# Gate-up weights by quarters of their columns, a later long convolution, decays and betas by transfers, and TensorE's usual end without a jump

## What is computed

```python
a = _rmsnorm(x, norm_mix);  proj = a @ w_in                      # q k v, z, beta, a, glu, gates
# branch a: gated delta rule, 8 heads, per token
beta = sigmoid(beta_raw);  g = -exp(a_log) * softplus(a_raw + dt_bias)
gc = cumsum(g) in chunks;  decay = exp(gc_i - gc_j);  kb = k * beta
# branch b: depthwise convolution with 31 taps over 512 channels, layernorm, silu
x = x + (g_a * branch_a + g_b * branch_b) @ w_out
# mixture of experts, 32 experts, top 4 for each token
for e in range(N_EXPERTS):
    gu = hm @ w_gate_up[e] + b_gate_up[e]                        # 1024 x 2048
    gate = jnp.minimum(gu[:, :D_FF], 7.0);  up = jnp.clip(gu[:, D_FF:], -7.0, 7.0)
    hid = (up + 1.0) * (gate * jax.nn.sigmoid(1.702 * gate))
    out = out + gates[:, e:e+1] * (hid @ w_down[e] + b_down[e])   # 1024 x 1024
x = x + out
x = x + (p_l @ w_ple_proj) * sigmoid(_rmsnorm(x, norm_ple) @ w_ple_gate)
y = _rmsnorm(x, norm_final)
```

## Time and profile before

| | |
|---|---|
| median of 3 runs | 1425.36 us (1422.98 to 1426.63) |
| profiled execution | 1425.09 us, its span 1423.0 us |
| PE busy | 1331.9 us (94%) |
| DVE, ACT, POOL busy | 456.7, 283.5, 27.9 us |
| moved | 463.23 MB, 326 GB/s over the span |

### The profile page before, as it was taken

How to read it: one execution, slowest core, us unless ns; L and a number is a source line. 1 busy time by engine, 2 the same in 40 slices (tenths; PEclk the granted TensorE clock), 3 DMA queues, 4 the chain that set the end, 5 groups by cost and what they waited for, 6 DMA issues and landing times.

```text
span 1423.0 us, 21274 instructions
## 1 busy us (share of the span) xinstructions
PE 1331.9 (94%) x8377; PEld 750.6 (53%) x8377; DVE 456.7 (32%) x1075; ACT 283.5 (20%) x609; POOL 27.9 (2%) x68
## 2 busy tenths in 40 slices
PE   8999899999999999999989889898898989989987
PEld 6877676778885443543433425334243443535455
DVE  3666868662235120220211202112020220202224
ACT  4645453534022100100100001000010000101024
POOL 3000000000000000000000000000000000000000
PEclk9999999999999999999999999999999999999999
DMA  7425244554868999999999999999999999999941
GB/s 219 138 90 154 91 125 148 152 209 126 323 217 351 402 420 422 420 421 420 422 420 420 421 422 421 421 421 421 421 421 421 420 415 420 421 422 421 419 154 31
DMA packets 123131, 463.23 MB, mean 326 GB/s; under 512 B 11141, under 2 KB 70046, under 8 KB 75310
## 3 DMA queue, kind: packets, MB, share of 16 engines
q1 hardware_dynamic: 106837, 452.99, 79.8%
q10 hardware_dynamic: 16193, 8.84, 2.2%
HBM read 455.78 MB, written 6.68 MB: 325 GB/s over the span
## 4 chain that ended last, share of the span: by engine, by line
PE 63%; DMA 15%; SPq 11%; DVE 5%; issue 3%; ACT 2%; ACTq 0%; POOL 0%; DVEq 0%; POOLq 0%
PE bank L1213 16%; PE bank L1260 12%; DMA ring<-in_w_gate_up 12%; SPq L622 11%; PE bank L1020 10%; PE bank L1152 5%; PE bank L1281 4%; PE bank L1067 3%; PE bank L1101 2%; PE bank L1335 2%; DMA late<-in_w_gate_up 2%; DMA dedicated<-in_w_gate_up 2%; PE bank L1199 1%; DVE lent L2010 1%; PE bank L1238 1%
## 5 line engine op out<-in xcount | busy, mean ns | idle before, releaser
L1213 PE MATMUL bank<-ring,lent 128*64 128x512 f32 (+1 forms) x1832 | 379.1, 595 | 44.1 <-DMA ring<-in_w_gate_up 44.1
L1213 PEld LDWEIGHTS bank<-ring,lent 128*64 128x64 f32 (+1 forms) x1832 | 121.8, 131 | 275.7 <-issue 275.2
L1020 PE MATMUL bank<-lent,ring 128*128 128x264 f32 x896 | 229.0, 397 | 5.1 <-DVE big L2030 1.6
L1260 PE MATMUL bank<-ring,lent 128*64 128x512 f32 (+1 forms) x928 | 184.3, 595 | 0.0
L1020 PEld LDWEIGHTS bank<-lent,ring 128*128 128x128 f32 x896 | 161.7, 191 | 40.4 <-issue 10.2
L2182 DVE TENSOR_SCALAR big<-bank 128x512 f32<-128x512 f32 x32 | 20.6, 686 | 409.2 <-PE bank L1213 409.2
L1260 PEld LDWEIGHTS bank<-ring,lent 128*64 128x64 f32 (+1 forms) x928 | 56.4, 129 | 106.8 <-issue 101.3
L1692 ACT ACTIVATE big<-big 128x512 f32<-128x512 f32 x32 | 19.5, 630 | 468.0 <-DVE big L2182 468.0
L1152 PEld LDWEIGHTS bank<-st,big 88*128 88x128 f32 x768 | 87.0, 192 | 13.6 <-issue 12.2
L1152 PE MATMUL bank<-st,big 88*128 88x128 f32 x768 | 90.3, 277 | 0.6 <-ACT pair_space L1689 0.5
L2200 DVE TENSOR_TENSOR xT<-xT,bank 128x264 f32<-128x264 f32 x128 | 55.0, 429 | 101.8 <-PE bank L1281 100.3
(11 more groups left out here) (436 smaller groups left out, 1352.3 us busy)
## 6 DMA issues: line engine op xcount, KB each, us to landing
ring<-in_w_gate_up SPq DMA_DIRECT2D x205, 1024.0 KB, 21.8
ring<-in_w_down SPq DMA_DIRECT2D x100, 1024.0 KB, 23.5
ring<-in_w_in SPq DMA_DIRECT2D x28, 1024.0 KB, 5.6
dedicated<-in_w_gate_up SPq DMA_DIRECT2D x13, 1024.0 KB, 23.8
dedicated<-in_w_down SPq DMA_DIRECT2D x9, 1024.0 KB, 24.1
late<-in_w_gate_up SPq DMA_DIRECT2D x8, 1024.0 KB, 23.0
outputs<-in_w_gate_up SPq DMA_DIRECT2D x7, 1024.0 KB, 26.4
lent<-in_w_gate_up SPq DMA_DIRECT2D x7, 1024.0 KB, 23.6
```

What stands on the lines that cost most here:

```text
L1020: last = mm(b[:, 0:T], w[:, k, o:o + P], aT[:, k, :], start=k == 0, stop=k == KD - 1)
L1213: last = mm(bank[t][lo:hi, :], x_slots[:, c, lo:hi], w, start=False, stop=c == KD - 1)
L1260: last = mm(bank[4 + t][lo:hi, :], hT[:, m, lo:hi], w, start=m == 0, stop=m == KD - 1)
```

## The change

1. **Quarters.** The host lays `w_gate_up` out so that chunk c = 2q + half holds, for four blocks of 128 contraction rows, the 256 gate and 256 up columns of quarter q. The chunk is still 1 MB, in rows of 8 KB. Chunk pair c now adds into bank q only, and quarter q is complete after two pairs. DVE and ACT work on quarters of 256 columns as they become complete, and PE transposes them between the pairs (`hidden_rows`). The scatter of the previous group moves from behind the gather to behind pairs 0 and 1. In the first group `x_ready` 2 is awaited at c = 1, not at c = 4.
2. **Places.** The first quarter's values are written early, so the two once-used places now hold chunks 2 and 3, and chunks 12 and 13 lie in the ring.
3. **Decays and betas.** `bcast` and `sel8` are gone. ACT stores the rows to DRAM once (slot 19) and reads them back spread over the partitions, two transfers for each pair of heads, issued in slot 24 and, for the next pair, in step `dt4` (`spread_rows`).
4. **Long convolution.** Taps come at 1 a slot up to slot 96 and at 2 a slot from there, its mean is asked for in slot 150 (`CONF_END` 50).
5. **End of PE.** The condition is turned round: the usual case is the body of the If, with `last_scatter` and the gate products (`ending`) in it. The last scatter uses eight different banks and starts when the first half of the last outputs is copied.
6. POOL clears `DT` and `Dm` for g < 2 only. `keep_warm` in the last group shrinks from 9 products to 2.

```diff
-BEFORE = {20: [17], 21: [18], 25: [3, 4], 26: [7, 8], 32: [0, 1], 33: [2, 5], 34: [6, 19]}
+BEFORE = {20: [17], 21: [18], 25: [13, 4], 26: [7, 8], 32: [0, 1], 33: [12, 5], 34: [6, 19]}
-SCATTER_BANKS = [4, 5, 6, 7, 2, 3, 6, 7]
+SCATTER_BANKS = [4, 5, 6, 7, 4, 5, 6, 7]
+LAST_BANKS = [1, 6, 7, 0, 2, 3, 4, 5]
-CONF_ROWS, TAILS, CONF_END = 22, 51, 48
+CONF_ROWS, TAILS, CONF_END = 22, 51, 50
-TAPS_FROM = 14
+TAPS_FROM, TAPS_DENSE_FROM = 14, 96
-        due += 4
+        due += 3 if x < TAPS_DENSE_FROM else 6
+        for i, name in zip((2, 3), ONCE):
+            j = home_of.index(name)
+            home_of[i], home_of[j] = home_of[j], home_of[i]
@@ PE, a group @@
+                    q, half = divmod(c, 2)
+                    for k in range(4):
                         for i, (x, lo, hi) in enumerate(tiles):
-                            w = weights(sems, n, 2 * c + x, t * 512)
-                            last = mm(bank[t][lo:hi, :], x_slots[:, c, lo:hi], w, start=False, stop=c == KD - 1)
+                            w = weights(sems, n, 2 * c + x, k * 512)
+                            last = mm(bank[q][lo:hi, :], x_slots[:, 4 * half + k, lo:hi], w, start=False,
+                                      stop=half == 1 and k == 3)
+                    if not first and c < 2:
+                        if c == 0:
+                            pe.wait_ge(sm["y_ready"], n * 2)
+                        scatter(sm, n - 1, 4 * c, 4 * c + 4)
...
+                    if half == 1 and c > 1:
+                        hidden_rows(sm, n, q - 1)
...
+                if not first:
+                    pe.wait_ge(sm["sc_added"], n * KD)
                 if not last_one:
                     gather(sm, n + 1)
                 elif end:
-                    pe.wait_ge(sm["y_ready"], n * 2)
-                    keep_warm(bank[4], 9)
+                    keep_warm(bank[4], 2)
+                hidden_rows(sm, n, 3)
+                gated_by_slot(sm, n)
@@ PE, the end @@
-            with pe.If(most > CAP):
+            with pe.If(most < CAP + 1):
                 last_scatter(first, GROUPS)
+                ending()
+            with pe.Else():
...
@@ ACT @@
+            def spread_rows(g):
+                betas = work[g % 2][10]
+                act.wait_ge(rows_stored, 16)
+                if g:
+                    act.wait_ge(s["sscaled"], 2 * g)
+                    act.wait_ge(s["kbg_ready"], 2 * g)
+                if g >= 2:
+                    wait_drained(act, f"o.{g - 2}")
+                for dst, x, done in ((eg, 1, decays_spread), (betas, 0, betas_spread)):
+                    src = head_rows[2 * g:2 * g + 2, x, :].unsqueeze(0).broadcast_to([P, 2, T])
+                    act.dma_start(dst, src).then_inc(done, 16)
-                    for j in range(2):
-                        b = to_drain(act, name(f"bcg{j}"))
-                        act.wait_ge(s["dec_diff"], 4 * g + 2 * j + 2)
-                        out_of(A(eg[:, j, :], b[:, 0:T], ACT.Exp), name(f"bcg{j}"))
+                    act.wait_ge(s["dec_diff"], 4 * g + 4)
+                    tell(A(eg[:], eg[:], ACT.Exp))
@@ DVE, a group @@
+                for q in range(4):
+                    g, u, gs = quarter(gbuf, q), quarter(ubuf, q), quarter(gsig, q)
+                    dve.wait_ge(sm["chunk_used"], at * RING + 4 * (q + 1))
+                    v.tensor_scalar(g, bank[q][:, 0:QUARTER_COLS], LIMIT, None, ALU.min).then_inc(sm["gate_in"], 1)
+                    then(v.tensor_scalar(u, bank[q][:, QUARTER_COLS:512], LIMIT, -LIMIT, ALU.min, ALU.max))
+                    dve.wait_ge(sm["gate_sig"], n * 4 + (q + 1))
+                    then(v.tensor_tensor(gs, gs, g, ALU.mult))
+                    v.scalar_tensor_tensor(g, u, 1.0, gs, ALU.add, ALU.mult).then_inc(sm["hid"], 1)
```

More of the change, by code:

```diff
@@ L1284, in last_scatter @@
             def last_scatter(sm, end):
-                pe.wait_ge(sm["y_ready"], end * 2)
                 pe.wait_ge(sm["spread"], end)
-                pe.wait_ge(sm["sc_added"], (end - 1) * KD)
-                scatter(sm, end - 1, 0, 6)
-                pe.wait_ge(sm["sc_added"], (end - 1) * KD + 4)
-                scatter(sm, end - 1, 6, 8)
+                pe.wait_ge(sm["h_ready"], end * 4)
+                pe.wait_ge(s["bd_added"], KD)
+                for i in range(KD):
+                    if i in (0, 4):
+                        pe.wait_ge(sm["y_ready"], end * 2 - (1 if i == 0 else 0))
+                    mm(bank[LAST_BANKS[i]][:, 0:T], y[:, i * P:(i + 1) * P], spread,
+                       start=True, stop=True).then_inc(sm["sc_filled"], 1)
             def gates_to_rows():
@@ L1536, in gdn_step @@
                     out_of(x, name(step))
+                    if step == "dt4" and g < 3:
+                        spread_rows(g + 1)
                 elif step == "adl":
@@ L2173, in group @@
                     make_selector(sm, eye_order, after, pos + 2)
+                if not first:
+                    add_back(sm, n - 1, SCATTER_BANKS)
                 if end:
-                    dve.wait_ge(sm["sc_added"], n * KD - KD)
-                    for i in range(KD):
-                        dve.wait_ge(s["bd_filled"], i + 1)
-                        v.tensor_tensor(xT[:, i, :], xT[:, i, :], bank[6 + i % 2][:, 0:T], ALU.add).then_inc(s["bd_added"], 1)
-                    dve.wait_ge(s["bd_added"], KD)
@@ L2190, in group @@
-                assert own[0] == PER
-                if not first:
-                    add_back(sm, n - 1, 0, KD)
+                    dve.wait_ge(sm["sc_added"], n * KD)
+                for q in range(4):
+                    g, u, gs = quarter(gbuf, q), quarter(ubuf, q), quarter(gsig, q)
[5 more added lines that the diff above has]
+                    v.scalar_tensor_tensor(g, u, 1.0, gs, ALU.add, ALU.mult).then_inc(sm["hid"], 1)
+                    if end:
+                        for i in (2 * q, 2 * q + 1):
+                            dve.wait_ge(s["bd_filled"], i + 1)
+                            v.tensor_tensor(xT[:, i, :], xT[:, i, :], bank[6 + i % 2][:, 0:T], ALU.add).then_inc(s["bd_added"], 1)
@@ L2194, in group, with add_back @@
+                assert own[0] == PER
+                if end:
+                    dve.wait_ge(s["bd_added"], KD)
                 dve.wait_ge(sm["pt_filled"], n + 1)
                 v.tensor_copy(spread, bank[2][0:SLOTS, 0:T]).then_inc(sm["spread"], 1)
[L2197 to L2198 removed]
+            def add_back(sm, n, banks):
+                for i in range(KD):
                     dve.wait_ge(sm["sc_filled"], n * KD + (i + 1))
[L2200 removed]
+                    v.tensor_tensor(xT[:, i, :], xT[:, i, :], bank[banks[i]][:, 0:T], ALU.add).then_inc(sm["sc_added"], 1)
```

273 lines of the change are left out of this document (125 added, 148 removed).

## The result

The changed kernel takes 1438.5 us (median of 4 runs, 1437.4 to 1442.1) against 1425.1 us, a ratio of 1.0095 with an interval of 1.0083 to 1.0107. It is 13.4 us slower, where 6.8 us faster was forecast. Its profiled execution takes 1439.2 us with a span of 1437.5 us, 14.5 us more than the span of before.

A forecast was written before the change was run, and what follows sets the result against it. Transfers were taken to set the experts' pace, about 59.8 us a group. Terms -8.6 + 2.8 - 0.9 = -6.7 us took the span from 1423.0 to 1416.3, forecast 1418.6 us, range 1413.5 to 1423.5 for 8 in 10.

The forecast's parts named there:

- (a): When PE starts on the experts counts in full, since all places are full and DMA waits for PE to free one.
- (b): Idle DMA time in the first expert group, before the queue has built up, counts in full.
- The first group, +2.8: Opening expert group: 4.1 us of added DMA idle time, less a 1.3 us gap that goes; bounds +1.5 and +4.1.
- The 4.1 us for pair 1: Opening group: pair 1 frees no place, so the next issues wait 3.6 us for pair 2, plus 0.5 us.
- The short gap at 476 to 480 us: First group: a DMA gap worth 1.3 us should go, as chunks 12 and 13 now free places.
- The first part, -0.9: Work ahead of the experts, with 32 PE instructions gone and taps moved: -0.9 us, bounds -7.1 and +3.
- PE will only wait longer: First part: with its products removed PE waits longer for ACT; gain 0.2 us for the first pair, 0 for the others.
- The taps: Long convolution in the first part: fewer early taps -0.8 us, mean not waiting -0.7, denser taps in slots 120 to 129 +0.7.
- The end, -8.6: Behind the last expert transfer: gate products start at 1370.9 in place of 1379.5, with the last w_ple_gate chunk as the floor.
- Half clock at the gate products: Rival: PE idles before the gate products and its clock falls, +2.4 us, 1421.0; chance 0.18.
- PE's removed work counts: Rival in the first part: ACT was itself held by PE, so up to 7.1 us go; half gives 1415; chance 0.12.
- PE's group passes the pace of the transfers: Rival: scatter and transposes between pairs lengthen each of some 15 groups; 8 us a group gives +22, 1441; chance 0.04.

The follow-up runs named there:

- experiment 6: Changed kernel with opening group's transposes behind its pairs, rows spread by products and the old long-convolution timetable: 1424.8 us, ratio 0.9994 to the kernel before.
- Experiment 1: Changed kernel, but in the opening group the first three quarters' transposes stand behind the eighth gate-up pair: 1429.2 us, ratio 1.0038 to the kernel before.
- experiment 2: Changed kernel plus 12 unread DVE operations, 5 us in all, behind the ordering of the experts: 1442.1 us.
- experiment 3: Changed kernel with decays and betas spread by 16 PE products again, no transfers for them: 1434.6 us, ratio 1.0077 to the kernel before.
- experiment 4: Changed kernel, rows still spread by transfers, plus unread PE products of the removed products' size in their old slots: 1434.0 us, ratio 1.0056 to the kernel before.
- experiment 8: Kernel before plus quarters and new ending, the opening group's first two transposes ahead of the gather: 1421.7 us, ratio 0.9974 to the kernel before.
- experiment 9: Kernel of experiment 8, but gate blocks wait for their own chunks of w_ple_gate (last two pairs share one wait): 1414.7 us, ratio 0.9911 to the kernel before.
- experiment 11: Kernel of experiment 8 with PE's old If and Else at the end: 1421.5 us against 1421.7.
- experiment 12: Kernel of experiment 9 with PE's old If and Else at the end: 1419.2 us against 1414.7.
- 10: Changed kernel with PE's old If and Else at the end: 1437.4 us against 1438.5.

## Why the prediction was wrong

*What bounds the kernel*: right. Transfers at 421 GB/s set the middle, and (a) the start of the experts and (b) idle DMA time in the first group are what counts. The failures are both in these two.

*The first group, +2.8.* The step that failed is the overlap in the opening group: the new transposes between the pairs were taken to find their quarter ready, and a wait there had no term. I asked what pair 1 frees, and didn't ask what stands in DVE's queue ahead of the first quarter. The 4.1 us for pair 1 are right (4.2 in experiment 6). The short gap at 476 to 480 us did not go there either. What was left out is the wait of 10.26 us behind 15.7 us of ordering, and the half clock behind it (2.6 us). Experiment 1 gives 8.2 us of the span back, 9.4 at the last landing, and experiment 2 returns 4.8 of 5.05 us.

*The first part, -0.9, measured +7.0.* (3.1 to 7.6 in the four profiles with this first part.) The waits came as forecast: 3.28 us near 141 us where 1.19 stood, 3.69 near 213. The step that failed is "PE will only wait longer". I priced the longer wait at nothing, while the prediction itself had a row in which the clock falls in a wait, and used it for the end only. Experiments 3 and 4: 1.9 to 6.4 us by the profile, 3.9 and 4.5 us by the medians. The taps are mis-sized, and smaller: +1.5 us (experiments 3 and 4 against 8 and 9), against 0.7 for the denser taps less 1.5 for waits that should go.

*The end, -8.6.* In a kernel whose transfers are nearly on time (experiment 8) the gate products start at 1372.73, 6.6 us before 1379.37 and at the landing, as the step has it. Which part earns it is another matter. The down products end at 1364.86 there and at 1368.43 before: quarters give 3.6 us and not 5.5, since the last down pair waits for a landing that comes later than forecast. From there to the gate products it was 10.9 us before. With the new last scatter (eight banks, an earlier start) and the old control flow it is 8.6 us (experiment 11) and 8.5 (experiment 12), so that scatter gives 2.3. With the new flow and no wait for `w_ple_gate` it is 4.4 (experiment 9). So the removed jump, forecast at 2.28 us and 2.7 us of half clock, is worth 4.05 us (the chain before has another 1.22 us of "issue" in front of the first two scatter products, which the forecast left out), but under 1 us while `w_ple_gate` is awaited as a whole. Counted from the start of the last down pair to the gate products, the four kernels give: old flow 12.3 us with the common wait and 12.2 with one for each chunk, new flow 11.5 and 8.1 (experiments 11, 12, 8, 9).

By the Trainium skill (Runtime: NRT & Kernel Launch, Instruction fetch mechanics) a taken branch whose target isn't held already has to wait for a fetch. The trace agrees: 3.27 against 0.77 us in front of the scatter, and a packet of instructions in that gap in all three kernels with the jump, against one of ten without.

In the changed kernel the 8.6 us weren't given back. They were used up: the transfers came 21.4 us late, and the floor that the forecast named, the last landing, decided.

*Rivals.* "Half clock at the gate products" got 0.18. Of nine profiles with the wait of 3.3 us it fell in six (first 32 in 8.95 to 10.41 us), so it was the likelier case, and 1.7 to 3.1 us against 2.4 (7.28 at full clock). The fall at 1371.8, which the prediction compares with a wait for transfers, came in idle time behind the jump; the fall at 1392 us in the changed kernel came in such a wait. "PE's removed work counts" went the other way. "PE's group passes the pace of the transfers" didn't happen: 420 GB/s throughout. The true course, PE held up by DVE in the opening group, was no rival at all, though "each behind DVE or ACT" stood in one of them, applied to every group but not to the first. Upper bounds of +3 for the first part and +4.1 for the first group, with all else against it, reached 1426 and left 1438.5 out.

*What the 21.4 us are made of.* Summed in stretches of 4 us, the kernel after is 8.05 MB behind between 320 and 500 us. Up to 320 us it moved 1.61 MB more, but 2.18 MB of that are the spread rows (463.23 and 465.41 MB in all), so it was 0.57 MB behind in the rest. From 500 to 1320 us it lost 0.29 MB. Together 8.9 MB, or 21.2 us at 421 GB/s.

*What stays open.* No run showed why the clock falls at one place in one execution and not in the next.

## What to carry to other kernels

When a kernel is bound by transfers and PE's uses free the places, look at the opening round by itself: draw up for each engine what stands ahead of the first new piece of work, for its queue holds one-off work that later rounds don't have. Price an idle stretch of PE by the clock behind it, not at zero; a few products for nothing may be cheaper than none. And split a wait for several chunks into one for each before shortening the path in front of it: here the split alone gave 0.1 us of PE's path, the shorter path alone 0.7, and both gave 4.2.

## What the runs showed of the hardware

- Removed work can cost time. 16 products, in sum 7.1 us of PE by the forecast's count, were replaced by waiting, and the experts started 2 to 6 us later by the clock. Waits of 2.21, 2.71 and 3.69 us (near 73, 285 and 213 us) were each followed by products at half clock in the changed kernel, one of 3.28 us near 141 us was not. In experiments 1, 2 and 10 the wait near 141 us was the same, 3.27 us, and the clock from 139 to 150 us fell to 0.84. The length of the wait alone does not tell.
- The same instructions spread by 4.5 us at the start of the experts (439.58 to 444.05 in four profiles of the changed first part). With the first part of the kernel before it is 3.5 us (435.13 to 438.59 in seven). An effect of 1 or 2 us is not to be read from two profiles without looking at the clock in each.
- A jump of TensorE cost 4.05 us: 2.5 in front of the target's first product, with a 16 KB packet of instructions in that gap (in three of three kernels), and 1.6 in its first 16.
